# Expert choice before the dots, query units in another order, two gathers in front: one core, two-block model layer

## The reference

```python
def block(xt):                       # xt: 128 tokens, called for two halves
    q = (xt @ wq).reshape(-1, 8, 2, 128)
    s = jnp.einsum('thpc,hpnc->thpn', q, keys)          # 8 heads, 2 key sets of 128
    sv, si = lax.top_k(s, 16)
    cand = (sv[:, :, 0, :, None] + sv[:, :, 1, None, :]).reshape(-1, 8, 256)
    ...
    top_s, top_j = lax.top_k(cand, 16)
    eid = jnp.take_along_axis(cid, top_j, axis=-1)
    gate = jax.nn.softmax(top_s.astype(jnp.float32), axis=-1)
    ue = jnp.take(u, eid, axis=0)                       # u, v: 16384 x 2048
    act = jax.nn.gelu(jnp.einsum('thkd,td->thk', ue, xt).astype(jnp.float32), approximate=False)
    ve = jnp.take(v, eid, axis=0)
    return jnp.einsum('thk,thkd->td', (gate * act).astype(xt.dtype), ve)
```

## Time and profile before

| | |
|---|---|
| median of three runs | 2985.42 us (2985.19 to 2987.33) |
| profiled execution | 2984.02 us, its span 2982.3 us |
| busy: PE, DVE, ACT, POOL | 89%, 58%, 29%, 19% of the span |
| DMA | 862.07 MB, mean 289 GB/s |
| gathers (software queue) | 536.90 MB, 43.5% of 16 engines' span |
| chain that ended last | PE 60%, DMA 32% |
| v rows on PE, L2412 | 886.1 us busy, 284.8 us idle before them for DMA |
| dots, L1748 | 586.5 us busy, 495.4 us idle before them, 487.9 of it for DMA |

### The profile page before, as it was taken

One profiled execution on the slowest core, in us unless ns is written; L12 is line 12 of the kernel. 1 busy time (PEld: TensorE's weight loads), 2 busy tenths in 40 slices (PEclk: granted clock), 3 DMA queues, 4 the chain that ended last, 5 costly groups with the idle time before them and its releaser, 6 DMA issues.

```text
span 2982.3 us, 32510 instructions
## 1 busy us (share of the span) xinstructions
PE 2665.4 (89%) x12254; PEld 1898.3 (64%) x12254; DVE 1723.9 (58%) x2247; ACT 873.7 (29%) x977; POOL 556.0 (19%) x533
## 2 busy tenths in 40 slices
PE   8999999987777777777777799999999999999998
PEld 8999888632222222222222247998888888888887
DVE  6556658655555555555555454645665655655445
ACT  4333431111111011111111014534544444444434
POOL 0000004454334433343344330000000000000000
PEclk9999999999999999999999999999999999999999
DMA  7555578999999999999999995544464555555554
GB/s 266 186 179 161 183 268 342 399 421 421 421 421 422 422 422 422 422 422 422 422 422 422 421 382 180 172 162 161 155 221 155 188 185 194 184 188 191 188 193 155
DMA packets 222908, 862.07 MB, mean 289 GB/s; under 512 B 17745, under 2 KB 24289, under 8 KB 149857
## 3 DMA queue, kind: packets, MB, share of 16 engines
q0 software_dynamic: 73728, 536.90, 43.5%
q1 hardware_dynamic: 149088, 323.92, 32.3%
HBM read 858.65 MB, written 2.11 MB: 289 GB/s over the span
## 4 chain that ended last, share of the span: by engine, by line
PE 60%; DMA 32%; issue 3%; DVE 3%; ACT 1%; POOL 1%; POOLq 0%; DVEq 0%; ACTq 0%
DMA vb<-in_peer_v,vidx 29%; PE PS L567 11%; PE PS L2412 8%; PE PS L2647 7%; PE PS L571 5%; PE PS L598 4%; PE PS L602 4%; PE PS L600 4%; PE PS L617 4%; PE PS L621 4%; PE PS L619 4%; DMA ub<-in_peer_u,uidx 2%; PE PS L641 1%; DMA raw<-in_peer_v,vidx 1%; DVE wl L470 1%
## 5 line engine op out<-in xcount | busy, mean ns | idle before, releaser
L2412 PE MATMUL PS<-vb,diag 128*128 128x512 f32 x1920 | 886.1, 606 | 284.8 <-DMA vb<-in_peer_v,vidx 284.8
L470 DVE TENSOR_TENSOR wl<-raw,wh 128x2048 fp32r<-128x2048 f32 x259 | 593.7, 2292 | 619.6 <-ACT wh L465 619.2
L1748 DVE CUSTOM_DVE_ANT_0 ub<-ub,RES 128x2048 f32<-128x2048 f32 x256 | 586.5, 2292 | 495.4 <-DMA ub<-in_peer_u,uidx 487.9
L2412 PEld LDWEIGHTS PS<-vb,diag 128*128 128x128 f32 x1920 | 347.4, 190 | 822.7 <-issue 533.8
L465 ACT CAST wh<-raw 128x2048 fp32r<-128x2048 f32 x259 | 493.8, 1907 | 753.0 <-PE PS L571 256.5
L567 PE MATMUL PS<-XHL,wh 128*128 128x512 f32 x1376 | 432.2, 395 | 0.7 <-DVE wl L470 0.7
L889 POOL DMA_INDIRECT ub<-in_peer_u,uidx x256 | 281.3, 1099 | 574.4 <-DVE uidx L1732 462.3
L889 POOL DMA_INDIRECT vb<-in_peer_v,vidx x240 | 245.0, 1021 | 624.7 <-PE PS L2412 593.0
L598 PE MATMUL PS<-XHL,wh 128*128 128x256 f32 x1088 | 309.9, 285 | 0.6 <-DVE wl L470 0.6
L602 PE MATMUL PS<-XHL,wl 128*128 128x256 f32 x1088 | 307.8, 283 | 0.0
L600 PE MATMUL PS<-XHL,wh 128*128 128x256 f32 x1088 | 307.8, 283 | 0.0
(11 more groups left out here) (419 smaller groups left out, 2601.7 us busy)
## 6 DMA issues: line engine op xcount, KB each, us to landing
raw<-in_w_in SPq DMA_DIRECT2D x112, 1024.0 KB, 5.1
raw<-in_w_ffn_gate SPq DMA_DIRECT2D x44, 1024.0 KB, 5.1
raw<-in_w_ffn_up SPq DMA_DIRECT2D x44, 1024.0 KB, 5.2
raw<-in_w_ffn_down SPq DMA_DIRECT2D x44, 1024.0 KB, 4.8
raw<-in_w_out SPq DMA_DIRECT2D x32, 1024.0 KB, 5.1
raw<-in_peer_wq SPq DMA_DIRECT2D x10, 1024.0 KB, 10.0
wq_early<-in_peer_wq SPq DMA_DIRECT2D x6, 1024.0 KB, 7.4
ub<-in_peer_u,uidx POOLq DMA_INDIRECT x256
```

Of the source, the lines that this page charges most:

```text
L470: dve.tensor_tensor(wl[u % 2][:], raw[u][:], wh[u % 2][:].bitcast(F32), ALU.subtract).then_inc(lo_full[u % 2], 1)
L1748: dve.tensor_tensor_reduce(ub[k % RING][:], ub[k % RING][:], RES[:, tb, :], 1.0, 0.0, ALU.mult, ALU.add, dots[:, tb, k:k + 1]).then_inc(S. ...
L2412: m = pe.matmul(PS[:, 4 * tb + b, :], diag[:, k, :], vb[k % RING][:, b * W:(b + 1) * W], start=False, stop=False, skip_group_check=True)
```

## The change

Four places are edited. VectorE: in step 0 the choice for step 1 is no longer spread over the 16 dots: its first half stands ahead of dot 0, the rest between dots 0 to 3. TensorE: the scores of the second half of head 0 are made between the two tiles of a unit, and scores 2 and 3 after (1,1) instead of (1,0); ScalarE's copy for them waits for one unit more, since (1,0) now lies where it writes. SyncE: eight query units of slabs 1 and 2 have buffers of their own, and the loads of slab 3 and of the first two `w_in_2` units wait for smaller counts of `q_used`. GpSimd: the first two u gathers of step 2 stand ahead of all v gathers.

```diff
-    wq_early = [... for k, kb in enumerate((32, 48, 40, 56, 80, 88))]
+    wq_early = [... for k, kb in enumerate((112, 32, 48, 40, 120, 56, 80, 88))]
@@ def wq_buf(j, u)
-        if j == 1:
-            return wq_early[u]
-        if j == 2 and u < 2:
-            return wq_early[UNITS + u]
-        return raw[(u + 2) % UNITS]
+        if j < 3:
+            return wq_early[UNITS * (j - 1) + u]
+        return (raw[2], raw[3], wq_early[1], wq_early[2])[u]
@@ SyncE
-        for j in range(1, 4):
-            for u in range(UNITS):
-                if j == 1:
-                    sp.wait_ge(w_free[u // 2], S_IN2 * 2)
-                elif j == 2 and u < 2:
-                    sp.wait_ge(S.out_half, 2)
-                else:
-                    sp.wait_ge(q_used, UNITS * (j - 2) + u - 1 if j == 2 else (3, 4, 11, 12)[u])
-                sp.wait_ge(raw_whole[u], 16 * j)
-                sp.dma_start(wq_buf(j, u)[:], wq[...]).then_inc(raw_whole[u], 16)
+        def load_query(j, u, sem, value):
+            sp.wait_ge(sem, value)
+            sp.wait_ge(raw_whole[u], 16 * j)
+            sp.dma_start(wq_buf(j, u)[:], wq[...]).then_inc(raw_whole[u], 16)
+        load_query(1, 1, w_free[0], S_IN2 * 2)
+        load_query(1, 2, w_free[0], S_IN2 * 2)
+        load_query(1, 3, w_free[1], S_IN2 * 2)
+        load_query(2, 1, w_free[1], S_IN2 * 2)
+        load_query(2, 2, S.out_half, 2)
+        load_query(2, 3, S.out_half, 2)
+        load_query(1, 0, S.h_ready, 8)
+        load_query(2, 0, S.h_ready, 8)
+        for u, used in enumerate((3, 4, 6, 8)):
+            load_query(3, u, q_used, used)
         for u in range(2):
-            sp.wait_ge(q_used, UNITS * 4 - 1 + u)
+            sp.wait_ge(q_used, 9 + u)
             load_unit(sp, S_IN2, u, w_in2[...])
@@ GpSimd
+        wait_alone(pool, S.uidx_ready, 3, S.pool_passed)
+        u_row(2, 0, 0, False)
+        u_row(2, 0, 1, False)
         for k in range(RING):
             v_row(0, 0, k, True)
-        wait_alone(pool, S.uidx_ready, 3, S.pool_passed)
-        u_row(2, 0, 0, False)
-        between = {5: 1, 6: 2, 8: 3, 9: 4, 11: 5, 12: 6, 14: 7}
+        between = {6: 2, 8: 3, 9: 4, 11: 5, 12: 6, 14: 7}
@@ ScalarE, pq_head
-            act.wait_ge(q_used, UNITS)
+            act.wait_ge(q_used, UNITS + 1)
@@ VectorE
         dve.wait_ge(S.scores_cp, 2)
-        expert_step(0, 0, 0)
+        take_scores(1, 0)
+        keys_first()
+        keys_next()
+        pair_sums()
+        pairs_first(1)
+        dot_rows(0, 0, 0, 1)
+        pairs_next()
+        dot_rows(0, 0, 1, 2)
+        pair_places()
+        dot_rows(0, 0, 2, 3)
+        key_places()
+        dot_rows(0, 0, 3, 4)
+        experts_out(1)
+        dot_rows(0, 0, 4)
+        weights(0, 0)
@@ TensorE
-                if u == 0:
+                if u == (j == 1):
                     scores(2 * j)
                     scores(2 * j + 1)
...
-        q1_tile(2, 0)
+        q1_tile(2, 0, 0, UC)
         q0_turn(1)
+        q1_tile(2, 0, UC)
+        scores(1)
         q1_tile(2, 1).then_inc(q_used, 1)
-        scores(1)
```

More of the change, by code:

```diff
@@ L250, in build @@
     wl = [at(f"wl{k}", 48 + 8 * k, [UC, W], F32R) for k in range(2)]
-    wq_early = [at(f"wq_early{k}", kb, [UC, W]) for k, kb in enumerate((32, 48, 40, 56, 80, 88))]
+    wq_early = [at(f"wq_early{k}", kb, [UC, W]) for k, kb in enumerate((112, 32, 48, 40, 120, 56, 80, 88))]
     XHL = at("XHL", 64, [DC, 2, T], F32R)
@@ L785, in _ @@
             sp.dma_start(narrow(raw[u]), wq[:, c:c + 2 * UC, (u // 2) * 2 * P:(u // 2 + 1) * 2 * P]).then_inc(raw_whole[u], 16)
-        for j in range(1, 4):
-            for u in range(UNITS):
-                if j == 1:
-                    sp.wait_ge(w_free[u // 2], S_IN2 * 2)
-                elif j == 2 and u < 2:
-                    sp.wait_ge(S.out_half, 2)
-                else:
-                    sp.wait_ge(q_used, UNITS * (j - 2) + u - 1 if j == 2 else (3, 4, 11, 12)[u])
-                sp.wait_ge(raw_whole[u], 16 * j)
-                sp.dma_start(wq_buf(j, u)[:], wq[:, u * UC:(u + 1) * UC, j * W:(j + 1) * W]).then_inc(raw_whole[u], 16)
-        w_in2 = w_view(inp["w_in_2"])
+        def load_query(j, u, sem, value):
+            sp.wait_ge(sem, value)
+            sp.wait_ge(raw_whole[u], 16 * j)
+            sp.dma_start(wq_buf(j, u)[:], wq[:, u * UC:(u + 1) * UC, j * W:(j + 1) * W]).then_inc(raw_whole[u], 16)
+        w_in2 = w_view(inp["w_in_2"])
+        load_query(1, 1, w_free[0], S_IN2 * 2)
[8 more added lines that the diff above has]
+            load_query(3, u, q_used, used)
         for u in range(2):
-            sp.wait_ge(q_used, UNITS * 4 - 1 + u)
+            sp.wait_ge(q_used, 9 + u)
             load_unit(sp, S_IN2, u, w_in2[:, u * UC:(u + 1) * UC, 4 * W:5 * W])
@@ L2337, in q0_turn, with q1_tile @@
             m.then_inc(S.q0_ps, 1)
-        def q1_tile(u, t):
-            for c in range(2 * UC):
+        def q1_tile(u, t, c0=0, c1=2 * UC):
+            for c in range(c0, c1):
                 d = (u % 2) * 2 * UC + c
```

## The result

Over 20 runs of each the changed kernel takes 2989.62 us (2987.56 to 2993.7), the kernel before 2985.77 us (2983.15 to 2988.57). The ratio is 1.0014 (1.0008 to 1.0021): 3.9 us slower. The forecast was 2982.9, the range ended at 2988.5. Against the bound of 0.2% that the chances used it is "no change"; with 20 runs the difference is clear of zero.

What follows compares the result with a forecast made beforehand. DMA was taken to bound the kernel, with only capacity unused before 600 us to win. One more block by 560 gives -2.5 us, other terms 0: 2984.02 to 2981.5, plus 1.4 to the median, 2982.9; range 2978.5 to 2988.5.

Steps and rivals of the forecast that it cites:

- The bound: Expert stage: DMA at 422 GB/s from 600 to 1650 us decides; only capacity unused before 600 can change the time.
- VectorE's part: Step 0's dots on VectorE: dot 15 ends at 524.2 (520.6 to 527.8), 2.2 us later than before.
- Dots 4 to 6 find their rows landed: VectorE, step 0: these three dots run at 2.2 us each without waiting, from 488.7 to 495.4.
- The nine rows after it: VectorE, step 0: dots paced by the ring of four at 3.2 us a row, 29 us, ending at 524.2.
- The second choice's stretch: VectorE's dots interleaved with the next choice of experts: 3.2 us a row; no added lateness in the forecast.
- The blocks by 560: 1 MiB row gathers moved by DMA from 455 to 560: 36.8 against 35.8, 1.0 more, 2.5 us gained.
- GpSimd: ... v0 around 570.5: GpSimd's first v gather, behind two u gathers of step 2, issued around 570.5 instead of 567.56.
- Does the lead survive? At 583.3, when v4 may go: Fifth v gather at 583.3 as before: 45.5 blocks moved of 48 issued, so DMA has work and the lead stays.
- D: Rival: slower, 2989.9 us; landings of 9.0 us make VectorE late, first v gather at 578, about 4.5 us lost; chance 0.08.
- the signs: Readings to tell the cases apart: 500:540 near 400 GB/s, 531:560 below 414, first v gather 567 to 572, dot 15 520 to 528.
- C: Rival: no gain, 2985.4 us; SyncE's units only move the DMA hole from 500:531 to 531:560; chance 0.25.
- B: Rival: all DMA holes filled, gathers keep pace with dots, 7.5 us less, 2977.9 us; chance 0.15.

Runs made afterwards that it cites:

- e11: Changed kernel with GpSimd's order and VectorE's spread choice of before, and the first two w_in_2 loads at counts 12 and 13: 2983.77 us, ratio 0.9990.
- e2: Changed kernel with the choice of step 0 spread over the 16 dots again: 2988.94 us, ratio 1.0005.
- e3: Changed kernel with the first two w_in_2 loads at their old counts 15 and 16 again: 2987.61 us, ratio 1.0006.
- e12: Kernel before with only VectorE's step 0 of the changed kernel (choice ahead): 2986.57 us, ratio 1.0000.
- e4: Kernel before with only GpSimd's new order, two u gathers of step 2 ahead of the v gathers: 2988.45 us, ratio 1.0006.
- e1: Changed kernel with GpSimd's order of before, four v gathers ahead of the u gathers of step 2: 2985.57 us, ratio 0.9997.
- e9: Changed kernel with four u gathers of step 2 ahead of the v gathers instead of two: 2992.93 us, ratio 1.0023.
- e5: Changed kernel with GpSimd's order and VectorE's choice of before, leaving SyncE's and TensorE's part: 2984.80 us, ratio 0.9993.

## Why the prediction was wrong

**The bound was right.** From 650 to 1650 us both kernels move 422 GB/s, no TensorE wait for a query unit came, and the bytes moved by 650 us give each kernel's span within 1.3 us in twelve of the thirteen rows of the table (e11: 2.1). (The slices with 421 or 422 GB/s in the earlier trace rows are 15, not 14; no sum uses it.)

**VectorE's part, right in mechanism, too small.** Dot 0 (475.1 forecast, 475.27) and the numbers at 488.7 held. "Dots 4 to 6 find their rows landed" did not: dot 5 waited 1.37 us for its gather, and dot 6 ended at 497.2 instead of 495.4. The nine rows after it took 29.1 us, 3.2 each, as reckoned, with landings of 6.9 to 8.3 us. So dot 15 ended at 526.3 where I had 524.2 (520.6 to 527.8). The second choice's stretch added 0.7 us more, and dot 27 was 5.0 us late, not 2.2.

What made it late is shown in part. Without the row of dots (e2) dot 27 is as late, and with the w_in_2 loads after 560 (e3) 3.3 of the 5.0 us are gone: that points to landings beside SyncE's loads. But e12, the row of dots with SyncE's loads of before, has dot 15 at 522.8 and dot 27 at 560.6, and e4, whose code up to there is that of before, has 521.9 and 561.15. With some 2 us from profile to profile, the share of each stays open.

**The blocks by 560: at the lower end.** I reckoned 1.0 block more (0 to 2). From 455 to 560 the kernel after moved 37.5 MB, as before: no lead. The 1.2 blocks in flight were right; GpSimd had issued 29 gathers instead of 30, since VectorE was 5.0 us late. SyncE's last load, issued at 524.4, had landed at 541.4; from then on only gathers came, one every 3.3 us (541.52 to 557.92, five steps), and 540:560 fell to 324 GB/s, the rate that I had written down as 328.

**"GpSimd: ... v0 around 570.5": the step that failed.** v0 went at 574.75, 7.2 us later than before and 4.3 later than forecast. Of the 4.3, 2.8 are dot 29, for which the second u gather waits (its issue at 571.8 instead of 569); the rest is that this issue was held inside the next dot and took 2.6 us. The runs show which of the two changes costs: with dots as late but v first (e1) v0 is only 1.3 us late, since in the kernel before it waited for the query units until 567.56; the two gathers in front add 5.9 us. With nearly the dots of before and two u gathers in front (e4) it is 3.7 us late. That v0's landing would lengthen I had nowhere: it took 9.8 us (577.05 to 586.8) against 7.4 before, behind two more u blocks.

**"Does the lead survive? At 583.3, when v4 may go": wrong, and this carries the sign.** I left v4 at the time of before, though v4 needs the first v row, which needs v0. It went 10.5 us later. In between DMA had eight SyncE, 34 u and four v blocks, gain and bias, and no more: it ran dry at 593, and then GpSimd issued v4, v5 and v6 3.4 us apart, the pace of TensorE's rows; the next u gather followed only at 601.9. 590:605 alone lost 15 x (421 - 289) = 1.98 MB, 4.7 us. With the block that didn't come (2.5 us) and 0.9 us in the other windows, this is the way from the forecast -2.5 us to the +5.6 us of the profile.

**The rivals.** D had this chain: first v row 8.6 us late (9.4), v4 at 592 (593.8), 4.5 us lost (3.9). That its numbers for these fit so well is in part luck: it had dot 29 ending near 577 (570.7) and v0 at 578 (574.75), both too late, and a landing of v0 that is shorter than before instead of longer. Its condition, v0 about 8 us late, was not quite met (7.2), and the loss was there. I gave it 0.08, since it asked for every landing at 9.0 us; in fact 4.3 us of lateness at dot 15 was enough, and in e4 the order of the queue alone, without the early loads, cost 3.9 us of bytes in its profile (1.6 us in the medians, not clear of zero). The range should have reached to it. Of the signs, those for dot 15, for 500:540 and for 531:560 came as the forecast had them; v0 past 572 and the hole after 590 were the ones that told. C happened too, in 540:560. B did not happen: with the hole in 500:540 filled another opened.

**What holds a gather.** The Trainium skill, page SBUF — State Buffer, section "Who interferes with whom", states that a VectorE instruction with two inputs in SBUF contends with a GpSimd one that reads SBUF, and that the later one waits for the whole of the other. The trace agrees: the six issues from 561.42 each start inside a dot, end 0.8 us after it and take 1.91 to 2.92 us, where one beside no dot takes 0.94. Five of the six stand before v0 in the one queue. The one-transfer fit of the Trainium skill, page DMA: Bandwidth & Descriptors, section "Anatomy of one DMA — SWDGE (gpsimd) path", gives an estimate of 4.4 us for a block, far from v0's landing of 9.8 us behind other gathers; the measurement decides.

## What to carry to other kernels

In a stage bound by DMA, count the bytes moved up to the point from which the rate is steady; here it followed the spans of thirteen profiles. When one queue feeds two consumers, what must come first is the transfer whose buffer releases the next ones: here each gather put in front of it to use idle DMA delayed the whole chain, by its wait, its issue and its place in the transfer queue. And when a step is moved in front of another, every later time that hangs on the second must be moved in the sum, not only its own.

## What the runs showed that I had not expected

v0 took 9.5 to 10.3 us from the end of its issue to its use in all seven profiles with one to four u gathers ahead (577.05 to 586.82 in the kernel after; in e9 582.23 to 592.52), 7.4 in the kernel before.

TensorE's clock was lower at the first v rows. After idling 12.55 us its granted clock was 0.50, the lower level of 1.2 GHz, in 580:590, and 0.82 on average in 590:595, in the kernel after:

```profile
580.00:590.00 10.00, 3.18 (x4) 1.51 (x5) 3.84 (x12) 1.22 (x5) 1.51 (x2) 0.50 1.01 425
590.00:595.00 5.00, 5.00 (x11) 2.06 (x10) 0.00 (x0) 0.40 (x1) 0.94 (x1) 0.82 0.65 270
```

The kernel before, after idling 3.46 us, has 0.68 at its first v row:

```profile
575.00:580.00 5.00, 2.60 (x3) 1.17 (x4) 0.18 (x1) 4.99 (x16) 1.52 (x2) 0.68 1.01 429
```

In e5, where it idled 2.59 us before the first v row, the same column has 1.00; in e12, after the same 2.59 us, 0.76. So the length of this one wait does not decide it. First e5, then e12:

```profile
575.00:580.00 5.00, 3.25 (x8) 1.61 (x9) 0.17 (x1) 4.99 (x15) 2.08 (x3) 1.00 0.99 385
```

```profile
575.00:580.00 5.00, 2.97 (x4) 1.28 (x5) 1.11 (x3) 4.97 (x15) 2.69 (x2) 0.76 1.03 415
```

v4 was issued 6.95 us after the first v row's start in the kernel after (586.82 to 593.77), 5.9 us in the kernel before, and 4.5 us in e5 (576.75 to 581.23). So of the 10.5 us by which v4 came later than before at most 1.05 us lies in this stretch, and the other 9.4 in the first v row; at the full clock of e5 v4 could have gone 2.5 us sooner. No run shows what that is worth in time.
